# The first expert index from the two maxima, two ring buffers opened by the first output half, and the late half of an output projection ahead of a head's query and scores

## The chip, the cores and the metric

The kernel runs as one program on one core of a Trainium2 chip. Its engines are TensorE (PE, matrix products into the accumulation memory PSUM), VectorE (DVE), ScalarE (ACT), GpSimd (POOL) and SyncE (SP), each with its own queue of instructions that it works through strictly in order; they wait for one another on semaphores. Sixteen DMA engines carry the transfers. The metric is the device time of one execution in microseconds, the median of several runs.

## The reference

Two transformer blocks over 256 tokens of 1024 numbers, in float32. The end of the second one is what the change touches: a cross attention over a memory, its output projection, and a product-key expert layer.

```python
x = x + memory_cross_attention(h, m, ...)       # ends in  o @ w_o   (the stage "xo")
h = rmsnorm(x, norm_ffn_g)
def token_chunk(xc):                            # 128 tokens at a time
    q = (xc @ w_q).reshape(128, 8, 2, 128)      # 8 heads, two half queries
    s = einsum("thpd,hpnd->thpn", q, subkeys)   # 128 scores for each half
    s1, i1 = top_k(s[:, :, 0], 16)
    s2, i2 = top_k(s[:, :, 1], 16)
    cand_s = s1[..., :, None] + s2[..., None, :]        # 256 sums
    cand_i = i1[..., :, None] * 128 + i2[..., None, :]
    top_s, top_pos = top_k(cand_s, 16)
    e = take_along_axis(cand_i, top_pos)        # 16 experts of 16384
    g = softmax(top_s)
    a = gelu(einsum("td,thkd->thk", xc, w_down[e]))
    return einsum("thk,thkd->td", g * a, w_up[e])
```

The largest of the 256 sums is always the sum of the two largest scores, so its index is the pair of their indices.

## The kernel before

All products of the dense stages are made from split operands (a high and a low part, three products for one). The 256 tokens are two halves of 128, m = 0 and m = 1. The expert layer is 16 steps `it`, eight heads of the first half and then eight of the second; each step has 16 picks. A pick is a number n = 16 it + k, 256 in all. For each pick GpSimd issues one gather (`indirect_dma_start`, line 2711): 128 tokens fetch one row of 2048 numbers each (the expert's down and up vectors), 1.05 MB, into one of a ring of buffers R. Three things are then done with a gathered buffer, two buffers (one group g) at a time:

- `dot_rows` on VectorE multiplies the down half with the token's row XN and sums (instruction `CUSTOM_DVE_ANT_0`, line 2497);
- ScalarE takes the GELU (`act_d`, line 1595), VectorE multiplies with the gate (`coef`, line 2506), and ScalarE makes a diagonal matrix of it (`DIAG`, line 1607);
- TensorE adds diagonal times up half to the output (`sums`, line 1167) and raises `up_done`.

`free_slot(n)` has GpSimd wait before gather n. The table `OPENED` names the picks that take a buffer for the first time, with the semaphore count that says that its old content is read; all other picks reuse the buffer of an earlier pick and wait for `up_done` of that one. Picks 0 to 7 are in `OPENED`; pick 8 reuses the buffer of pick 0 and so on, so that pick 19 waits for the sum of pick 12. Seven buffers go round until pick 21 opens another one.

The beginning of step 0 lies among the last dense work, and its order is written out by hand on each engine. The names in it: `side("xo", AXo, g, 1)` is half g of the output projection of the second token half (line 1019, 12 matrix products), it needs the low part AXo_lo of the attention result (VectorE, line 2291, after AXo_hi by ScalarE); `query(j, 0, ...)` is the query of head j (line 641, eight products for each part named) and `head_scores(j, 0)` on TensorE its scores (line 656, label SK,QP), which first wait until ScalarE has copied the query out (`queries(j, 0)`, QP, line 1615); `head_scores` on ScalarE copies the scores into SC (line 1582; line 1619 for head 0). On VectorE `first_eight` and `second_eight` pick the experts of step 0 and write their indices IDX (line 2411), `top_a` to `top_h` do that for the later steps, and `residual_side`, `gain_side` and `mean_side` are the norm of the second token half. On ScalarE `square_side`, `gate_exp`, `gelu`, `diagonals` and `activate` (the last two together) belong to the same.

Of the kernel before, what the change touches and what calls it, by code (L numbers as in the profile page):

```python
# [17 lines left out]
T = 256  # L18
# [152 lines left out]
def build(nc, weights, vecs, consts, xT, x, mem, rows, gws, gbs, subkeys, experts, out):  # L171
    ctx = ExitStack()
    with ctx:
# [115 lines left out]
        for n, u in enumerate((1, 2, 5, 6, 12)):  # L289
            OPENED[3 + n] = (u, XO_END)  # L290
# [284 lines left out]
        def _(pe):  # L575
# [575 lines left out]
            query(1, 0, (1,))  # L1151
            head_scores(1, 0)
            has_lo(pe, *values_parts(1))
            side("xo", AXo, 0, 1)
            side("xo", AXo, 1, 1)
            query(2, 0)
# [56 lines left out]
        def _(act):  # L1213
# [400 lines left out]
            def queries(j, m):  # L1614
# [4 lines left out]
            drain_aux(act.activation(SC[:, 0, 0:2, :], v3(batch(act, *scores_of(0, 0))[:, 0:T], 2), ACT.Copy),  # L1619
                      *scores_of(0, 0))  # L1620
# [5 lines left out]
            queries(1, 0)  # L1626
            head_scores(1, 0)
            gate_exp(0)
            warm(ACT.Gelu_apprx_tanh)
            gelu(0, 0)  # L1630
            queries(2, 0)
            diagonals(0, 0)
            head_scores(2, 0)
            square_side("xo", 3, 1, 0)
# [60 lines left out]
        def _(dve):  # L1695
# [723 lines left out]
            def decode_eight(ks, side):  # L2419
# [19 lines left out]
                index(0, ks)  # L2439
# [10 lines left out]
            def first_eight():  # L2450

                wait_aux(dve, *scores_of(0, 0))
                for vals, idx, src, work in firsts(0):
                    st.do(dve.max(vals[:, 0:8], src))
                st.sync()
                for vals, idx, src, work in firsts(0):
                    st.do(dve.max_index(idx[:, 0:8], vals[:, 0:8], src))
                st.then(sums_of(c8[:, 0, :].rearrange("p (a b) -> p a b", b=8), low8, low8))
                st.do(dve.tensor_copy(tif[:, :, 0:8], ti[:, :, 0:8]))
                st.then(dve.max(cv[:, 0:8], c8[:, 0, :]))  # L2460
                st.then(dve.max_index(cp[:, 0, 0:8], cv[:, 0:8], c8[:, 0, :]))
                decode_eight(low8, 8)

            def second_eight():

                st.do(dve.match_replace(c8[:, 1, :], cv[:, 0:8], c8[:, 0, :], LOWEST))
                for vals, idx, src, work in firsts(0):
                    st.do(dve.match_replace(work, vals[:, 0:8], src, LOWEST))
                st.sync()
# [45 lines left out]
            top_a(1)  # L2515
            top_b(1)
# [5 lines left out]
            coefs(0, 1)  # L2522
            gain_side(1, 1, 0)
# [164 lines left out]
        def _(pool):  # L2688
# [14 lines left out]
            for it in range(16):  # L2703
                pool.wait_ge(idx_ready, it + 2 if it else 1)
                for k in range(TOPK):
                    if it == 0 and k == 8:
                        pool.wait_ge(idx_ready, 2)
# [93 lines left out]
```

## Time and profile before

| | |
|---|---|
| median of the runs (lowest, highest) | 1336.57 us (1336.38, 1337.8) |
| profiled execution, first to last instruction | 1332.9 us |
| TensorE busy | 1212.4 us (91%) |
| VectorE busy | 935.0 us (70%) |
| ScalarE busy | 544.3 us (41%) |
| GpSimd busy | 292.8 us (22%) |
| DMA | 396.71 MB, mean 298 GB/s |
| chain that ended last | PE 56%, DMA 32%, DVE 6%, ACT 3% |
| mean granted TensorE clock | 0.986 of full speed |

No time of its own is given for the profiled execution but its span of 1332.9 us; the median lies 3.67 us above that span. Busy shares are means over a program with very different stages; the stages are told apart by the slices of the page's second part and by windows. The chain is followed back from the last instruction, at each step to what released it.

### The profile page before, as it was taken

How to read it: one execution, taken by the hardware profiler on the slowest of the kernel's cores; microseconds unless marked ns; L12 is line 12 of the kernel's file. 1: busy time of each engine (PE TensorE's matmuls, PEld its weight loads, DVE VectorE, ACT ScalarE, POOL GpSimd, SP SyncE). 2: the span in 40 equal slices, each digit the busy share in tenths (PEclk: the TensorE clock that was granted, in tenths of full speed). 3: DMA queues.
4: the chain of work that ended last, by engine and by line, in shares of the span. 5: the costliest groups of instructions: out<-in, count | busy, mean ns of one | idle time of the engine just before them, and what ended most of it. 6: DMA issues, size and time to landing. Idle time of an engine off the chain costs nothing.

```text
span 1332.9 us, 17294 instructions
## 1 busy us (share of the span) xinstructions
PE 1212.4 (91%) x6222; PEld 874.1 (66%) x6222; DVE 935.0 (70%) x1853; ACT 544.3 (41%) x977; POOL 292.8 (22%) x261
## 2 busy tenths in 40 slices
PE   9999999999999999999998999899877877877776
PEld 9999998988888899999774554444422323332332
DVE  6865758887764675557687787776777777777655
ACT  5843225556643446645643333233322222222312
POOL 0000000000000000000034455444544444544430
PEclk9999999999999999999999999999999999999999
DMA  7553225555565654447779999999999999999996
GB/s 281 190 184 133 95 102 211 194 172 189 190 227 199 206 177 172 143 171 288 281 278 420 420 418 420 418 420 419 420 420 419 420 421 419 420 419 421 420 420 267
DMA packets 55927, 396.71 MB, mean 298 GB/s; under 512 B 6320, under 2 KB 6320, under 8 KB 8624
## 3 DMA queue, kind: packets, MB, share of 16 engines
q0 software_dynamic: 36864, 268.45, 48.7%
q1 hardware_dynamic: 17136, 119.16, 25.0%
q10 hardware_dynamic: 1856, 8.13, 1.7%
q8 instruction: 47, 0.77, 0.2%
q14 instruction: 24, 0.20, 0.0%
HBM read 394.67 MB, written 1.05 MB: 297 GB/s over the span
## 4 chain that ended last, share of the span: by engine, by line
PE 56%; DMA 32%; DVE 6%; ACT 3%; issue 2%; POOL 2%; DVEq 0%; ACTq 0%; POOLq 0%
DMA R<-experts,IDX 32%; PE ps L591 19%; PE ps L674 10%; PE ps L1167 8%; PE ps L904 4%; PE ps L603 3%; PE ps L906 2%; PE ps L641 2%; POOL R L2711 2%; PE ps L1019 1%; DVE R L2497 1%; PE ps L799 1%; PE ps L787 1%; ACT DIAG L1607 1%; PE ps L1046 1%
## 5 line engine op out<-in xcount | busy, mean ns | idle before, releaser
L1167 PE MATMUL ps<-R,DIAG 128*128 128x512 f32 x1020 | 482.4, 620 | 105.2 <-ACT DIAG L1607 105.2
L1167 PEld LDWEIGHTS ps<-R,DIAG 128*128 128x128 f32 x1020 | 190.2, 195 | 372.9 <-issue 196.2
L2497 DVE CUSTOM_DVE_ANT_0 R<-R,XN 128x1024 f32<-128x1024 f32 x256 | 313.5, 1226 | 142.8 <-DMA R<-experts,IDX 142.2
L2711 POOL DMA_INDIRECT R<-experts,IDX x256 | 291.5, 1139 | 531.7 <-PE ps L1167 273.0
L1738 DVE TENSOR_TENSOR w_lo<-raw,w_hi 128x1024 fp32r<-128x1024 f32 x204 | 241.7, 1220 | 78.5 <-ACT w_hi L1220 74.3
L1220 ACT ACTIVATE w_hi<-raw 128x1024 fp32r<-128x1024 f32 x203 | 204.7, 1051 | 77.4 <-DMA raw<-weights 77.4
L1595 ACT ACTIVATE act_d<-dots,rst 128x2 f32<-128x2 f32 (+1 forms) x130 | 38.5, 296 | 329.9 <-DVE dots L2497 329.8
L1607 ACT ACTIVATE DIAG<-con,coef 128x128 f32<-128x128 f32 x255 | 88.6, 394 | 122.2 <-DVE coef L2506 120.9
L591 PE MATMUL ps<-opA_lo,w_hi 128*128 128x256 f32 x384 | 110.6, 288 | 0.5 <-issue 0.5
L591 PE MATMUL ps<-opA_hi,w_lo 128*128 128x256 f32 x384 | 108.5, 283 | 0.0
L591 PE MATMUL ps<-opA_hi,w_hi 128*128 128x256 f32 x384 | 108.5, 283 | 0.0
L591 PE MATMUL ps<-both_C,w_hi 128*128 128x256 f32 x576 | 105.4, 284 | 1.3 <-DVE MB L1958 1.0
L2691 POOL TENSOR_SCALAR_AFFINE_SELECT WS<-WS 128x1024 f32<-128x1024 f32 x1 | 1.1, 1085 | 466.7 <-DMA BS<-gbs 466.7
L591 PEld LDWEIGHTS ps<-both_C,w_hi 128*128 128x128 f32 x576 | 90.3, 192 | 3.2 <-DVE MB L1958 1.8
L904 PE MATMUL ps<-both_C,w_hi 128*128 128x512 f32 x256 | 89.0, 392 | 0.9 <-DVE both_C L1708 0.9
L591 PE MATMUL ps<-both_C,w_lo 128*128 128x256 f32 x288 | 81.5, 283 | 0.0
L591 PEld LDWEIGHTS ps<-opA_lo,w_hi 128*128 128x128 f32 x384 | 73.5, 191 | 1.7 <-issue 0.8
L591 PEld LDWEIGHTS ps<-opA_hi,w_lo 128*128 128x128 f32 x384 | 73.6, 192 | 0.0
L591 PEld LDWEIGHTS ps<-opA_hi,w_hi 128*128 128x128 f32 x384 | 73.5, 191 | 0.0
L906 PE MATMUL ps<-both_C,w_lo 128*128 128x256 f32 x256 | 71.7, 280 | 0.0
L904 PEld LDWEIGHTS ps<-both_C,w_hi 128*128 128x128 f32 x256 | 47.9, 187 | 11.6 <-issue 1.2
L591 PEld LDWEIGHTS ps<-both_C,w_lo 128*128 128x128 f32 x288 | 55.3, 192 | 0.0
(396 smaller groups left out, 1757.1 us busy)
## 6 DMA issues: line engine op xcount, KB each, us to landing
raw<-weights SPq DMA_DIRECT2D x103, 1024.0 KB, 4.9
PQW<-weights SPq DMA_DIRECT2D x6, 1024.0 KB, 8.5
R<-experts,IDX POOLq DMA_INDIRECT x256, 29.9
LNR<-rows ACTq DMA_DIRECT2D x3, 1024.0 KB, 4.9
raw<-weights SPq DMA_DIRECT2D x4, 512.0 KB, 8.7
XF<-xT SPq DMA_DIRECT2D x2, 512.0 KB, 5.7
MEM<-mem ACTq DMA_DIRECT2D x1, 1024.0 KB, 7.8
XR<-x ACTq DMA_DIRECT2D x1, 1024.0 KB, 5.0
```

The source lines that it names most:

```text
L591: mm = pe.matmul(dst[:, c * T:(c + 1) * T], a[:, i, c * P:(c + 1) * P], b[:, k0 + i, :], start=(first and c == 0 and i == ks[0] and n == 0 ...
L603: mm = pe.matmul(dst[:, m * 256:(m + 1) * 256], b[:, k0 + i, m * P:(m + 1) * P], a[:, i, :], start=(first and m == 0 and i == ks[0] and n ...
L674: mm = pe.matmul(psum[:, 4 + 2 * g + m, :], o[:, 4 * k + i, m * P:(m + 1) * P], a[:, 2 * i:2 * i + 2, :].rearrange("p a b -> p (a b)"), st ...
L904: pe.matmul(dst[:, c, :], w_up[:, k, c * P:(c + 1) * P], both_C[:, :, k, :], start=(k == 0), stop=False, skip_group_check=True)
L906: mm = pe.matmul(dst[:, c, 0:T], w_down[:, k, c * P:(c + 1) * P], both_C[:, 0, k, :], start=False, stop=(k == 7), skip_group_check=True)
L1167: mm = pe.matmul(psum[:, 4 + 2 * m + n, :], DIAG[:, k, :], rows_[:, D + n * 512:D + (n + 1) * 512], start=(it % 8 == 0 and k == 0), stop=True,
L1220: act.activation(w_hi[s][:, 4 * h:4 * h + 4, :], raw[s][:, 4 * h:4 * h + 4, :], ACT.Copy).then_inc(hi_ready, 1)
L1595: act.activation(act_d[:, par, k0:k1], dots[:, par, k0:k1], ACT.Gelu_apprx_tanh, scale=rst[:, it // 8:it // 8 + 1]).then_inc(gelu_done, 1)
L1607: ins = act.activation(DIAG[:, k, :], ident, ACT.Copy, scale=coef[:, par, k:k + 1])
L1738: dve.tensor_tensor(w_lo[w][:, ks, :], raw[w][:, ks, :], w_hi[w][:, ks, :], ALU.subtract).then_inc(lo_ready, 1)
L2497: dve.tensor_tensor_reduce(out=rows_[:, 0:D], in0=rows_[:, 0:D], in1=XN[:, m, :], scale=1.0, scalar=0.0, op0=ALU.mult, op1=ALU.add, accum_ ...
L2711: pool.indirect_dma_start(out=R[u][:, :], out_offset=None, in_=experts, in_offset=bass.IndirectOffsetOnAxis(ap=IDX[:, it, k:k + 1], axis=0 ...
```

## The change

Four edits, all at the start of the expert layer. (1) `first_eight` reads the scores of head 0 directly from PSUM, where before ScalarE copied them to SC; that copy is gone. It writes the index of pick 0 from the two maxima's indices at once and those of picks 1 to 7 afterwards, and takes the two `match_replace` of `second_eight` over. GpSimd waits for the one index before pick 0, for the seven before pick 1, and for the eight before pick 8. (2) `OPENED`: the buffers in units 1 and 5 open with the first half of the "xo" projection, and take picks 3 and 4; units 2, 6 and 12 still wait for both halves. (3) On TensorE both halves `side("xo", AXo, 0, 1)` and `side("xo", AXo, 1, 1)` come ahead of the second part of head 1's query and of its scores. (4) ScalarE does `gate_exp(0)`, `gelu(0, 0)` and a `square_side` before it copies head 1's query, and VectorE does `top_a(1)` and `top_b(1)` after the first two pairs of dot products, where they stood ahead of both.

```diff
-        for n, u in enumerate((1, 2, 5, 6, 12)):
-            OPENED[3 + n] = (u, XO_END)
+        FIRST_XO_END = half_end(BLOCK["xo"])
+        s0 = BLOCK["xo"] % 4
+        for n, u in enumerate((s0, 4 + s0)):
+            OPENED[3 + n] = (u, FIRST_XO_END)
+        for n, u in enumerate((s0 + 1, 5 + s0, 12)):
+            OPENED[5 + n] = (u, XO_END)
...
             query(1, 0, (0,))
             cross_values(1)
-            query(1, 0, (1,))
-            head_scores(1, 0)
             has_lo(pe, *values_parts(1))
             side("xo", AXo, 0, 1)
             side("xo", AXo, 1, 1)
+            query(1, 0, (1,))
+            head_scores(1, 0)
             query(2, 0)
             query(3, 0, (0,))
             head_scores(2, 0)
...
             queries(0, 0)
-            drain_aux(act.activation(SC[:, 0, 0:2, :], v3(batch(act, *scores_of(0, 0))[:, 0:T], 2), ACT.Copy),
-                      *scores_of(0, 0))
...
             values_hi(1)
-            queries(1, 0)
-            head_scores(1, 0)
             gate_exp(0)
             warm(ACT.Gelu_apprx_tanh)
             gelu(0, 0)
+            square_side("xo", 3, 1, 0)
+            queries(1, 0)
+            diagonals(0, 0)
+            head_scores(1, 0)
             queries(2, 0)
-            diagonals(0, 0)
             head_scores(2, 0)
-            square_side("xo", 3, 1, 0)
             activate(0, 1)
...
             def first_eight():
-                wait_aux(dve, *scores_of(0, 0))
-                for vals, idx, src, work in firsts(0):
+                pa = batch(dve, *scores_of(0, 0))
+                lists = [(vals, idx, pa[:, q * NK:(q + 1) * NK], work)
+                         for q, (vals, idx, _, work) in enumerate(firsts(0))]
+                for vals, idx, src, work in lists:
...
+                st.do(dve.tensor_copy(tif[:, :, 0:8], ti[:, :, 0:8]))
                 st.then(sums_of(c8[:, 0, :].rearrange("p (a b) -> p a b", b=8), low8, low8))
+                largest = slice(0, 1)
+                dve.scalar_tensor_tensor(out=IDX[:, 0, largest], in0=tif[:, 0, largest], scalar=float(NK),
+                                         in1=tif[:, 1, largest], op0=ALU.mult, op1=ALU.add
+                                         ).then_inc(idx_ready, 1)
...
-                decode_eight(low8, 8)
+                decode_eight(low8, 8, slice(1, 8))
+                for vals, idx, src, work in lists:
+                    st.do(dve.match_replace(work, vals[:, 0:8], src, LOWEST))
+                st.sync()
+                drain_aux(dve.engine_nop(), *scores_of(0, 0))
...
-            top_a(1)
-            top_b(1)
             dot_rows(0, 0)
             residual_side("xo", 3, 1, 0)
             coefs(0, 0)
             dot_rows(0, 1)
             residual_side("xo", 4, 1, 1)
             coefs(0, 1)
+            top_a(1)
+            top_b(1)
             gain_side(1, 1, 0)
...
-                pool.wait_ge(idx_ready, it + 2 if it else 1)
+                pool.wait_ge(idx_ready, it + 3 if it else 1)
                 for k in range(TOPK):
-                    if it == 0 and k == 8:
-                        pool.wait_ge(idx_ready, 2)
+                    if it == 0 and k in (1, 8):
+                        pool.wait_ge(idx_ready, 2 if k == 1 else 3)
```

On VectorE the order after the gates GW of step 0 was this: MAX to MAX_INDEX are `top_a(1)` and `top_b(1)`, `ISA R,dots` is a dot product with a gathered buffer.

```order
L2490 TENSOR_SCALAR GW<-gx,gs 128x16
L2359 MAX tv<-SC 128x8 x2
L2362 MATCH_REPLACE sW<-tv,SC 128x128 x2
L2368 MAX tv<-sW 128x8
...
L2372 MAX_INDEX ti<-tv,sW 128x8 x2
L2497 ISA R_150,dots<-R_150,XN 128x1024
...
L2506 TENSOR_TENSOR coef<-act_d,GW 128x2
...
L2247 TENSOR_TENSOR XN<-XR,LNR 128x512 x2
L2378 CAST tif<-ti 128x32
```

With the change the same place reads:

```order
L2500 TENSOR_SCALAR GW<-gx,gs 128x16
L2507 ISA R_150,dots<-R_150,XN 128x1024
...
L2507 ISA R_140,dots<-R_140,XN 128x1024
L2507 ISA dots 128x1
L2244 TENSOR_TENSOR XR<-XR,ps 128x512
L2516 TENSOR_TENSOR coef<-act_d,GW 128x2
L2361 MAX tv<-SC 128x8 x2
L2364 MATCH_REPLACE sW<-tv,SC 128x128 x2
...
L2249 TENSOR_TENSOR XN<-XR,LNR 128x512 x2
```

The selection work of step 1 moved behind the coefficients of the second pair (the second `coef`, the last one shown ahead of MAX). On ScalarE, from the high part of the attention result on, the order was:

```order
L1534 ACTIVATE AXo_hi<-ps 128x4x128
L1615 ACTIVATE QP<-ps 128x2x128
L1582 ACTIVATE SC<-ps,rst 128x256
L1587 ACT_TABLE_LOAD
L1587 ACTIVATE gx,gs<-cv,gs,rst 128x16
L1384 ACT_TABLE_LOAD
L1384 ACTIVATE lbd<-con 128x1
L1595 ACTIVATE act_d<-dots,rst 128x2
```

and it is now:

```order
L1538 ACTIVATE AXo_hi<-ps 128x4x128
L1591 ACT_TABLE_LOAD
L1591 ACTIVATE gx,gs<-cv,gs,rst 128x16
L1388 ACT_TABLE_LOAD
L1388 ACTIVATE lbd<-con 128x1
L1599 ACTIVATE act_d<-dots,rst 128x2
L1490 ACTIVATE XS,ssq<-XR 128x512
L1619 ACTIVATE QP<-ps 128x2x128
L1611 ACTIVATE DIAG<-con,coef 128x128 x2
L1586 ACTIVATE SC<-ps,rst 128x256
L1619 ACTIVATE QP<-ps 128x2x128
L1586 ACTIVATE SC<-ps,rst 128x256
```

The copy of head 1's query, QP, moved behind the first GELU (act_d) and a square (XS). On TensorE, after the attention values (XT,VX), only the place of head 1's second query part and scores differs; they now stand behind the last "xo" product and ahead of head 2's query (PQW_130):

```order
L1023 MATMUL ps<-w_hi_61,AXo_hi 128x512
L645 MATMUL ps<-H_129,raw_51 128x128 x8
L660 MATMUL ps<-SK,QP 128x128 x2
L645 MATMUL ps<-H_129,PQW_130 128x128 x16
L645 MATMUL ps<-H_129,PQW_131 128x128 x8
L660 MATMUL ps<-SK,QP 128x128 x2
L1171 MATMUL ps<-R_150,DIAG 128x512 x2
```

What moved there are eight products and two; the sums of pick 0 (R_150) stay behind all of them.

## Rows read from the trace of the kernel before

**Rows 1.** The page, its second part: GB/s moved in 40 equal slices.
```profile
GB/s 281 190 184 133 95 102 211 194 172 189 190 227 199 206 177 172 143 171 288 281 278 420 420 418 420 418 420 419 420 420 419 420 421 419 420 419 421 420 420 267
```

**Rows 2.** The page, DMA queues: packets, MB, share of 16 engines' span.
```profile
q0 software_dynamic: 36864, 268.45, 48.7%
```

**Rows 3.** The chain that ended last, its end: start us, us, what.
```profile
1290.64 33.21 DMA R<-experts,IDX
1323.87 1.23 DVE R L2497
```

**Rows 4.** Windows of one us: busy times of PE, PEld, DVE, ACT, POOL, clock, DMA share, GB/s.
```profile
676.00:677.00 1.00, 0.53 (x5) 0.40 (x4) 0.96 (x7) 0.38 (x1) 0.90 (x1) 1.00 0.72 131
...
685.00:686.00 1.00, 1.00 (x12) 1.00 (x11) 0.97 (x2) 0.00 (x0) 0.69 (x2) 1.00 0.64 221
```

**Rows 5.** Timeline of GpSimd: start us, us, line, what, idle before and releaser.
```profile
674.57 1.09 POOL L2711 DMA_INDIRECT R<-experts,IDX  x1 [206.22 <-DVE IDX L2411]
...
683.06 0.94 POOL L2711 DMA_INDIRECT R<-experts,IDX  x1 [4.92 <-PE ps L1019]
...
692.01 0.95 POOL L2711 DMA_INDIRECT R<-experts,IDX  x1 [1.60 <-PE ps L1167]
...
722.36 0.94 POOL L2711 DMA_INDIRECT R<-experts,IDX  x1 [2.57 <-PE ps L1167]
```

**Rows 6.** Timeline of VectorE: dot products that waited for their gather.
```profile
700.59 1.23 DVE L2497 CUSTOM_DVE_ANT_0 R<-R,XN 128x1024 f32<-128x1024 f32 x1 [0.63 <-DMA R<-experts,IDX]
...
730.52 1.23 DVE L2497 CUSTOM_DVE_ANT_0 R<-R,XN 128x1024 f32<-128x1024 f32 x1 [1.01 <-DMA R<-experts,IDX]
```

**Rows 7.** Timeline of VectorE from the first pick to the third pair.
```profile
670.35 0.49 DVE L2454 MAX8 tv<-SC 128x8 f32<-128x128 f32 x2 [1.58 <-ACT SC L1619]
...
671.22 0.28 DVE L2457 FIND_INDEX8 ti<-tv,SC 128x8 uint32<-128x128 f32 x1
...
674.12 0.17 DVE L2411 SCALAR_TENSOR_TENSOR IDX<-ef 128x8 uint32<-128x8 f32 x1
675.08 0.69 DVE L2291 TENSOR_TENSOR AXo_lo<-ps,AXo_hi 128x512 fp32r<-128x512 f32 x1 [0.80 <-ACT AXo_hi L1534]
...
682.41 0.49 DVE L2359 MAX8 tv<-SC 128x8 f32<-128x128 f32 x2 [0.20 <-DVE GW L2490]
...
685.28 1.23 DVE L2497 CUSTOM_DVE_ANT_0 R<-R,XN 128x1024 f32<-128x1024 f32 x1
...
691.38 0.16 DVE L2506 TENSOR_TENSOR coef<-act_d,GW 128x2 f32<-128x2 f32 x1
...
694.18 1.23 DVE L2497 CUSTOM_DVE_ANT_0 R<-R,XN 128x1024 f32<-128x1024 f32 x1
```

**Rows 8.** Timeline of ScalarE, from head 0's scores to head 3's.
```profile
669.94 0.39 ACT L1619 ACTIVATE SC<-ps 128x256 f32<-128x256 f32 x1 [0.80 <-PE ps L656]
...
687.76 0.30 ACT L1595 ACTIVATE act_d<-dots,rst 128x2 f32<-128x2 f32 x1 [6.11 <-DVE dots L2497]
...
689.56 0.62 ACT L1486 ACTIVATE XS<-XR 128x512 f32<-128x512 f32 x1
...
703.17 0.45 ACT L1582 ACTIVATE SC<-ps,rst 128x256 f32<-128x256 f32 x1
```

**Rows 9.** The chain that ended last, TensorE's pieces: start us, us, what.
```profile
677.32 5.49 PE ps L1019 x24
...
889.34 5.40 PE ps L1167 x8
```

**Rows 10.** Timeline of TensorE: queries (L641) and sums (L1167).
```profile
682.63 5.52 PE L641 MATMUL ps<-H,PQW 128*128 128x128 f32 x48
...
689.24 7.13 PE L1167 MATMUL ps<-R,DIAG 128*128 128x512 f32 x16 [0.15 <-ACT DIAG L1607]
...
698.15 3.70 PE L1167 MATMUL ps<-R,DIAG 128*128 128x512 f32 x8
...
709.66 3.70 PE L1167 MATMUL ps<-R,DIAG 128*128 128x512 f32 x8 [1.77 <-ACT DIAG L1607]
```

More of the change, by code:

```diff
@@ L2417, in top_g, with decode_eight @@
                 index(it, slice(0, 16))
-            def decode_eight(ks, side):
+            def decode_eight(ks, side, listed=None):
                 shape, bits = [P, 8, side], {8: 3, 16: 4}[side]
@@ L2438, in decode_eight @@
                 st.sync()
-                index(0, ks)
+                index(0, listed or ks)
             def sums_of(dst, rs, cs):
@@ L2450, in first_eight, with second_eight @@
             def first_eight():
-                wait_aux(dve, *scores_of(0, 0))
-                for vals, idx, src, work in firsts(0):
+                pa = batch(dve, *scores_of(0, 0))
+                lists = [(vals, idx, pa[:, q * NK:(q + 1) * NK], work)
+                         for q, (vals, idx, _, work) in enumerate(firsts(0))]
+                for vals, idx, src, work in lists:
                     st.do(dve.max(vals[:, 0:8], src))
                 st.sync()
-                for vals, idx, src, work in firsts(0):
+                for vals, idx, src, work in lists:
                     st.do(dve.max_index(idx[:, 0:8], vals[:, 0:8], src))
+                st.sync()
+                st.do(dve.tensor_copy(tif[:, :, 0:8], ti[:, :, 0:8]))
                 st.then(sums_of(c8[:, 0, :].rearrange("p (a b) -> p a b", b=8), low8, low8))
-                st.do(dve.tensor_copy(tif[:, :, 0:8], ti[:, :, 0:8]))
+                largest = slice(0, 1)
+                dve.scalar_tensor_tensor(out=IDX[:, 0, largest], in0=tif[:, 0, largest], scalar=float(NK),
+                                         in1=tif[:, 1, largest], op0=ALU.mult, op1=ALU.add
+                                         ).then_inc(idx_ready, 1)
                 st.then(dve.max(cv[:, 0:8], c8[:, 0, :]))
                 st.then(dve.max_index(cp[:, 0, 0:8], cv[:, 0:8], c8[:, 0, :]))
-                decode_eight(low8, 8)
-            def second_eight():
-                st.do(dve.match_replace(c8[:, 1, :], cv[:, 0:8], c8[:, 0, :], LOWEST))
-                for vals, idx, src, work in firsts(0):
+                decode_eight(low8, 8, slice(1, 8))
+                for vals, idx, src, work in lists:
                     st.do(dve.match_replace(work, vals[:, 0:8], src, LOWEST))
                 st.sync()
+                drain_aux(dve.engine_nop(), *scores_of(0, 0))
+            def second_eight():
+                st.then(dve.match_replace(c8[:, 1, :], cv[:, 0:8], c8[:, 0, :], LOWEST))
                 st.do(dve.tensor_copy(cand[:, 0:8, 0:8], c8[:, 1, :].rearrange("p (a b) -> p a b", b=8)))
```

## The prediction

> **What bounds the kernel now.** I read the slices first. From about the twenty-second on they stand at 418 to 421 GB/s [rows 1], which nothing earlier in the kernel reaches: from the expert layer's start to its end the DMA engines are full. The gathers' queue moves 268.45 MB [rows 2], 256 gathers of 1.05 MB; at 420 GB/s that is 639 us, 2.50 us for a gather. Then the end of the chain: the last gather is issued at 1290.64 and its dot product starts at 1323.87, 33.21 us of pure transfer [rows 3]. So the time is the moment when the gather stream starts, plus 639 us, plus every stretch in which the stream runs dry, plus a short tail. Ahead of the stream the chain is TensorE's, but only what moves the stream counts.
>
> The first window with gather traffic is 676 to 677, 131 GB/s [rows 4]; the first gather was issued at 674.57 [rows 5], so bytes move about 1.8 us after the issue. One gap follows, 221 GB/s in the window 685 to 686 [rows 4]: gathers 0 to 2 were out, and pick 3 was issued only at 683.06, after the "xo" projection [rows 5]. After that the stream lives off its ring. GpSimd waits for TensorE's sums before nearly every gather [rows 5], and how much reserve it has shows where a dot product waits for data: gather 19, issued at 722.36 [rows 5], landed just before 730.52 [rows 6], 8.16 us later. Gather 7 landed just before 700.59 [rows 6], so twelve gathers took 29.93 us, 2.494 each: no hole. What would the 8.16 us be at least, in an empty queue? For gather 0 they are 1.8 us to the first byte, and 1.05 MB have moved only after some 3.2 us more (131 GB/s in its first window), 5.0 us as the lower bound. From above: the dots of the second pair ran at 688.4 to 690.7 without a wait for data, which holds gather 3, issued at 683.06, under 6.5 us. I take 5.8, nearer the upper end, since the last of sixteen engines decides. The reserve at pick 19 is then 2.3 us (1.7 to 3.1). By the same reading picks 8 to 14 have more, and picks 15 and 17 about 0.3 us more.
>
> **The change at the front: 2.7 us earlier.** Without the copy of 0.39 us at 669.94 [rows 8] the maxima, which waited for it [rows 7], start at 669.96. The finds end 1.15 us after the maxima's start (671.22 + 0.28 against 670.35) [rows 7]; a cast, the sums and the one index instruction of 0.17 us follow, some 0.3 us ahead of it: the index at 671.4 instead of 674.12, gather 0 at 671.9 instead of 674.57 [rows 5]. The other seven indices come at about 673.9, gather 1 at 674.3, in time for the end of gather 0's bytes. Reading PSUM instead of SBUF I cost at nothing. The Trainium skill, "Perfetto Trace Analysis", Optimizing Scalar/DVE Operations, gives VectorE about 60 ns of overhead on SBUF and 125 ns on PSUM; by it the front would be some 0.3 us later, an estimate from that page, and the forecast the same.
>
> **The two buffers and the projection: one gap less.** AXo_lo is done at 675.77 (675.08 + 0.69) [rows 7], bound by ScalarE as before. TensorE starts "xo" at about 675.95, 1.4 us earlier than 677.32, and needs the same 5.49 us [rows 9]: first half done at 678.7, second at 681.4. Picks 3 and 4 go at 679 and 680.2, picks 5 to 7 from 681.7, with gathers 0 to 2 still moving. The gap at 685 goes, 0.2 to 0.7 us. If nothing else happened, the stream would be about 2.7 us ahead, a little more with the gap.
>
> **What pays for it: the sums of the first step come later.** I follow the three engines by their order.
> - VectorE: `second_eight` lost two match_replace, 0.5 us, and `top_a(1)`, `top_b(1)` (682.41 to 685.28, 2.87 us) stand no more ahead of the dots [rows 7]. The first dot starts at 681.9 instead of 685.28, the GELU at 687.76 - 3.4 = 684.4 [rows 8].
> - ScalarE: now the GELU, and then the square stand ahead of head 1's query copy. The square waits for the residual after the second dot, 684.2 + 0.7 = 684.9, and takes 0.7 us with its read-out (0.62 the instruction) [rows 8]. QP starts at 685.6, before at 676.2.
> - TensorE: "xo" ends at 681.4, the query part at 683.2, and then it stands until QP is done: head 1's scores at 686.05. Behind them are three query parts, 5.52 us [rows 10] less their overlap, so 5.4, and head 2's scores, 0.45 us each: 686.05 + 0.45 + 5.4 + 0.45 = 692.35 for the first sum, against 689.24 [rows 10]. **3.1 us later.**
> - The second pair: ScalarE's GELU of it stands behind its copy of head 2's scores, 691.9 + 0.8 + 0.4 = 693.1, and the coefficient comes at 693.4, not 691.38 [rows 7]. Behind that coefficient VectorE had 2.8 us of work until the third pair's dot at 694.18 [rows 7]; now it also has the 2.87 us. The third pair's dots start at 693.4 + 2.8 + 2.87 = 699.05, **4.9 us later**.
> - From dot to sum took 694.18 to 698.15 [rows 7, 10], of it 0.3 us waiting for data that now lie there: sums at 702.8, 4.65 later. The fourth pair waited 0.63 us for gather 7 [rows 6], which falls away: 4.0 later. ScalarE's copy of head 3's scores at 703.17 [rows 8] moves to 707.1, and from it a fixed series of table loads, root, exponential and GELU led to TensorE's sums at 709.66 [rows 8, 10], 6.49 us: now 713.6, **3.9 us later**.
> - From there to pick 12's sum TensorE is full (sums, query, sums, query), so pick 19 is issued at 722.36 + 3.9 = 726.3.
>
> **The sum.** Pick 19 lands at 726.3 + 5.8 = 732.1 instead of 730.5: 3.9 later less 2.3 reserve, **1.6 us later**, and the stream is dense behind it, since pick 21 opens another buffer and the reserve grows. The 2.7 us of the front are used up before: gather 8 waits for the first sum, 692.01 + 3.1 = 695.1 [rows 5], while gathers 0 to 7 are over by about 697 minus the engines' spread, so some engines stand empty. The same sum by the bounds of the floor is 3.9 - 3.1 = 0.8 and 3.9 - 1.7 = 2.2. An error of half a us in the 3.9 widens this to 0.3 to 2.7. Span: 1332.9 + 1.6 = 1334.5. The median lies 3.67 us above the span shown, so 1336.57 + 1.6 = 1338.2. What a measurement of this kernel can tell from no change is about 0.2%, 2.7 us; 1.6 us is within it.
>
> **Rivals.**
> - The head start arrives whole, -2.7 to -3.4 us, 1333.5. That needs picks 15 to 19 no later than now by 0.4 us, so an error of 4.3 us in the chain above. For it speaks that the first dots really come 3.4 us earlier. Against it, TensorE's wait for QP follows from the written order and leaves nothing to chance. The Trainium skill, "Perfetto Trace Analysis", Optimization Strategy, says to find the gaps of the saturated resource and to make what they depend on start sooner. Taken alone that is this case, and by it the time is 1333.5. Chance 0.12.
> - The sums come later, but by no more than 1.9 to 2.7 us at pick 19 (TensorE or ScalarE catch up, or the floor of a gather is nearer 5.0 us): the end moves by -0.4 to +0.3, 1336.5. Chance 0.2.
> - Slower beyond the bound: the shift at pick 19 passes 5.0 us, the point from which 5.0 - 2.3 = 2.7 is lost. One mechanism would do it. TensorE now stands idle twice in 12 us, 1.6 us before "xo" and 2.9 us before head 1's scores, and the clock row shows what a drop costs: at 889.34 eight sum products took 5.40 us [rows 9], where they take 3.70 [rows 10]. One such stretch in the dense part before pick 12 adds 1.7 us, 3.3 in all, 1339.9. The Trainium skill, "TensorE: Matmul & The Clock Gate", The HAM clock gate, says that activity releases the throttle and idleness brings it back; against it, no row before 840 us shows less than full clock, though TensorE waits there too (1.77 us at 709.66) [rows 10]. Without the clock, a restart of all sixteen engines at each hole (the ramp of rows 4) adds up to 0.5 us a hole. Chance together 0.23.
> - The forecast, +0.3 to +2.7 us: chance 0.45.
>
> **How the numbers follow.** Faster by over 0.2% is the first rival alone, 0.12. Slower by over 0.2% is the third with the upper rim of the forecast, 0.25. The rest, 0.63, is within 0.2%. The range must leave out no more than 2 in 10: from 1335.2, which cuts the first rival, to 1340.2, which holds the clock's case and cuts what is beyond.
>
> **What the next profile would show.** Right: the first gather issued at about 671.9, picks 3 and 4 near 679 and 680; TensorE's L660 for head 1 near 686.0 behind a wait of some 2.9 us for QP; the first sum near 692.3; the third pair's dots near 699; windows between 694 and 707 with less than 420 GB/s; pick 19 near 726.3. Wrong: if the first sum stands before 690, the order costs less than I say; if the windows after 677 are all full, the head start arrives; if the clock is under 1.00 before 730, the third rival holds; if gathers in an empty queue land in under 5 us, the reserve was larger.

## The result, and the profile after

The changed kernel took 1342.85 us in the median (1342.58 to 1343.23, 4 runs), the kernel before on the same chip 1336.53: a ratio of 1.0043 with an interval of 1.0031 to 1.0055, so 4.1 to 7.4 us slower. Forecast were 1338.2 us and a range up to 1340.2. The profiled execution spans 1341.5 us. All medians and ratios here are of fast runs; one execution of front_open, below, took 2680.8 us, twice the time, and is left out.

One thing has to be set right before the two traces are laid side by side. In the profile after, head 0's scores start at 670.87 us, in that of before they started at 669.19, though nothing ahead of them was changed. A second profile of the kernel before has them at 669.09, and over all 18 profiles of this study they start either at 668.8 to 669.4 (ten) or at 670.6 to 671.0 (eight), kernels before and after in both groups. So 1.68 us of the 8.6 us between the two spans are chance. It also explains about half of the 3.67 us by which the median of the kernel before stood above the span shown: the second profile, with the same span of 1332.9 us, took 1334.63 us itself, so both executions profiled were of the faster kind. From here on, times are compared **from the start of head 0's scores on TensorE** ("from the scores").

TensorE in the changed kernel, from its timeline (start us, us, line, what, count, idle time before and its releaser; L660 are a head's scores, L1023 "xo", L645 queries, L1171 sums; in the kernel before these were L656, L1019, L641 and L1167):

```profile
670.87 0.71 PE L660 MATMUL ps<-SK,QP 128*128 128x128 f32 x4 [0.47 <-ACT QP L1619]
...
677.57 0.50 PE L1023 MATMUL ps<-w_hi,AXo_lo 128*128 128x512 f32 x1 [1.54 <-DVEq L1718]
...
687.48 0.91 PE L660 MATMUL ps<-SK,QP 128*128 128x128 f32 x4 [2.39 <-ACT QP L1619]
688.18 7.00 PE L645 MATMUL ps<-H,PQW 128*128 128x128 f32 x48
...
695.47 7.03 PE L1171 MATMUL ps<-R,DIAG 128*128 128x512 f32 x16
...
716.65 3.70 PE L1171 MATMUL ps<-R,DIAG 128*128 128x512 f32 x8 [1.78 <-ACT DIAG L1611]
```

The two stands are there, 1.54 and 2.39 us. The 48 query products behind the second take 7.00 us; the same 48 took 5.52 before [rows 10]. The windows say why (us; busy of PE, PEld, DVE, ACT, POOL; granted clock, DMA share, GB/s):

```profile
687.00:688.00 1.00, 0.52 (x4) 0.52 (x5) 0.74 (x2) 1.00 (x5) 0.99 (x1) 0.93 1.00 418
688.00:689.00 1.00, 1.00 (x6) 1.00 (x6) 0.00 (x0) 0.49 (x2) 0.54 (x1) 0.50 0.99 418
...
690.00:691.00 1.00, 1.00 (x7) 1.00 (x7) 1.00 (x3) 0.00 (x0) 0.00 (x0) 0.50 0.97 410
```

The granted clock fell to 0.50, the lower of its two levels (1.2 GHz), right behind the stand. Scores to first sum: 24.60 us, before 20.05 (689.24 - 669.19) [rows 10].

GpSimd (gathers 0, 3, 8, 11 and 19) and VectorE (the first maxima, the first dot product, the first of the third pair, and that of pick 19):

```profile
673.60 1.09 POOL L2721 DMA_INDIRECT R<-experts,IDX  x1 [203.21 <-DVE IDX L2466]
...
680.86 0.94 POOL L2721 DMA_INDIRECT R<-experts,IDX  x1 [2.62 <-PE ps L1023]
...
698.13 0.94 POOL L2721 DMA_INDIRECT R<-experts,IDX  x1 [9.59 <-PE ps L1171]
...
708.11 1.50 POOL L2721 DMA_INDIRECT R<-experts,IDX  x1 [3.90 <-PE ps L1171]
...
729.35 0.94 POOL L2721 DMA_INDIRECT R<-experts,IDX  x1 [1.96 <-PE ps L1171]
```

```profile
671.62 0.50 DVE L2458 MAX8 tv<-ps 128x8 f32<-128x128 f32 x2 [1.16 <-PE ps L660]
...
683.42 1.22 DVE L2507 CUSTOM_DVE_ANT_0 R<-R,XN 128x1024 f32<-128x1024 f32 x1
...
702.17 1.22 DVE L2507 CUSTOM_DVE_ANT_0 R<-R,XN 128x1024 f32<-128x1024 f32 x1
...
737.49 1.23 DVE L2507 CUSTOM_DVE_ANT_0 R<-R,XN 128x1024 f32<-128x1024 f32 x1 [1.07 <-DMA R<-experts,IDX]
```

The first gather goes out 2.73 us after the scores, before 5.38 (674.57 - 669.19) [rows 5]: the head start is there, 2.65 us. Pick 19 goes out 58.48 us after them, before 53.17: 5.3 us later. The stream in windows of 4 us, first of the changed kernel, then of the kernel before:

```profile
692.00:696.00 4.00, 4.00 (x35) 3.76 (x34) 0.00 (x0) 0.66 (x2) 0.00 (x0) 1.00 1.01 426
696.00:700.00 4.00, 4.00 (x11) 1.80 (x10) 3.37 (x18) 1.69 (x6) 0.94 (x1) 1.00 0.37 102
700.00:704.00 4.00, 4.00 (x21) 2.61 (x20) 3.90 (x10) 0.00 (x0) 2.17 (x2) 1.00 0.86 303
...
708.00:712.00 4.00, 3.70 (x12) 1.85 (x11) 3.79 (x11) 2.72 (x6) 2.52 (x2) 1.00 0.56 178
...
724.00:728.00 4.00, 4.00 (x22) 2.74 (x21) 3.07 (x11) 0.85 (x3) 2.48 (x2) 1.00 0.99 358
728.00:732.00 4.00, 4.00 (x14) 2.03 (x13) 2.06 (x5) 0.99 (x3) 1.88 (x2) 1.00 0.94 358
```

```profile
696.00:700.00 4.00, 4.00 (x22) 2.65 (x21) 3.66 (x12) 1.37 (x4) 1.21 (x2) 1.00 1.01 426
700.00:704.00 4.00, 2.98 (x11) 1.59 (x10) 3.24 (x9) 1.71 (x5) 1.87 (x2) 1.00 1.00 416
...
708.00:712.00 4.00, 2.34 (x6) 1.14 (x7) 3.21 (x7) 1.85 (x5) 0.30 (x2) 1.00 1.02 424
```

The stream runs dry twice, behind gather 7 (pick 8 comes at 698.13) and behind gather 10 (pick 11 comes at 708.11), and is thin up to 736. From 676 to 744 the 17 windows of before sum to 6930 GB/s, those of after to 6081: 849 x 4 / 420 = 8.1 us of full stream less. By place: 1.0 us gained up to 696, then 4.2 lost by 704, 0.3 by 708, 2.3 by 712, 2.3 by 736. Less the 1.68 us of chance, and less the 0.35 us of bytes that the changed kernel moved ahead of 676 (147 GB/s from 675 to 676), it is 6.1, the size of the result. From 744 on both run at full rate until the last ten us.

### The profile page after: what moved, and what is told of

Its sections match the earlier page's. It is cut to its first block, busy times and chain, and to the rows that moved or that the text cites. A ratio compares the mean times of both kernels' runs of the same rounds, so it can differ in the third digit from the quotient of the medians.

```text
span 1341.5 us, 17294 instructions
## 1 busy us (share of the span) xinstructions
PE 1211.9 (90%) x6222; PEld 873.8 (65%) x6222; DVE 936.0 (70%) x1854; ACT 543.7 (41%) x976; POOL 290.2 (22%) x261
## 3 DMA queue, kind: packets, MB, share of 16 engines
HBM read 394.67 MB, written 1.05 MB: 295 GB/s over the span
## 4 chain that ended last, share of the span: by engine, by line
PE 57%; DMA 30%; DVE 7%; ACT 3%; issue 2%; POOL 0%; DVEq 0%; ACTq 0%; POOLq 0%
DMA R<-experts,IDX 30%; PE ps L595 19%; PE ps L678 10%; PE ps L1171 9%; PE ps L908 4%; PE ps L607 3%; PE ps L645 3%; PE ps L910 2%; DVE R L2507 1%; PE ps L803 1%; PE ps L1023 1%; PE ps L791 1%; ACT DIAG L1611 1%; PE ps L1050 1%; PE ps L1077 1%
## 5 line engine op out<-in xcount | busy, mean ns | idle before, releaser
L1171 PE MATMUL ps<-R,DIAG 128*128 128x512 f32 x1020 | 478.6, 615 | 110.7 <-ACT DIAG L1611 107.7
L1171 PEld LDWEIGHTS ps<-R,DIAG 128*128 128x128 f32 x1020 | 188.1, 194 | 376.8 <-issue 197.5
```

What stands on the lines that cost most here:

```text
L1171: mm = pe.matmul(psum[:, 4 + 2 * m + n, :], DIAG[:, k, :], rows_[:, D + n * 512:D + (n + 1) * 512], start=(it % 8 == 0 and k == 0), stop=True,
```

## The experiments

For every run two times are given, both from the scores: when pick 19 is issued, and when the last gather has landed (the last DMA row of the chain, its start plus its length). For the kernel before, profiled again (TensorE, GpSimd, and the chain's last piece of DMA), and for the changed kernel's chain:

```profile
669.09 0.71 PE L656 MATMUL ps<-SK,QP 128*128 128x128 f32 x4 [0.47 <-ACT QP L1615]
...
722.34 0.94 POOL L2711 DMA_INDIRECT R<-experts,IDX  x1 [2.57 <-PE ps L1167]
...
1290.42 33.35 DMA R<-experts,IDX
```

```profile
1299.03 33.36 DMA R<-experts,IDX
```

So 53.25 and 1323.77 - 669.09 = 654.68 for before; 58.48 and 1332.39 - 670.87 = 661.52 for the changed kernel. The others, in the order of pick 19 (shift against this second profile of before, us; ratio of times to before with its interval where timed in rounds):

| kernel | first sum | pick 19 | end | ratio |
|---|---|---|---|---|
| query_later | -0.6 | -3.0 | -2.3 | 0.9987 (0.9978, 0.9996) |
| front_open | -0.6 | -1.6 | -1.6 | 0.9987 (0.9978, 0.9996) |
| before_late | +1.7 | +0.5 | +0.3 | 1.0009 (1.0000, 1.0018) |
| old_pe_act | -0.8 | +0.8 | +1.3 | 1.0015 (1.0006, 1.0024) |
| mid_2us | 0.0 | +1.5 | +2.5 | 1.0016 (1.0006, 1.0025) |
| qp_first | +1.1 | +1.7 | +2.2 | 1.0012 (1.0003, 1.0021) |
| filled_short | +2.9 | +3.6 | +3.8 | 1.0030 (1.0020, 1.0039) |
| after_again | +2.9 | +3.6 | +4.7 | 1.0034 (1.0021, 1.0048) |
| mid_4us | 0.0 | +3.6 | +3.7 | 1.0030 (1.0019, 1.0041) |
| changed kernel | +4.6 | +5.2 | +6.8 | 1.0043 (1.0031, 1.0055) |
| filled | +4.7 | +5.4 | +5.9 | 1.0044 (1.0031, 1.0058) |
| orders_only | +5.4 | +6.0 | +6.4 | 1.0045 (1.0031, 1.0059) |

**before_again**: the kernel before, unchanged.

> The kernel before, unchanged, for a second profile. The profile shown of before had head 0's scores (TensorE, L656) at 669.19, that of the changed kernel at 670.87, although nothing ahead of them was changed. Theory A: that is a difference between executions; this profile has the scores anywhere from 669 to 671, a span near 1334.8, and a time near 1336.5. Theory B: the changed program itself is slower up to there; then the scores stand at 669.2 again. From the scores to the first sum 20.05 us by both.

Measured: one run of 1334.63 us, scores at 669.09, first sum 20.05 us after them. By itself it did not settle whether the 1.68 us were chance; it fell on the same side as the first profile. The later ones settled it: before_late and mid_4us, which are the kernel before up to that point, have 670.97 and 670.83, and the changed kernel's third and fourth profile 669.28 and 669.39. Theory A.

**front_open**: edits 1 and 2 without the orders. On TensorE, ScalarE and VectorE the changed kernel's new orders are put back, for example

```diff
             cross_values(1)
+            query(1, 0, (1,))
+            head_scores(1, 0)
             has_lo(pe, *values_parts(1))
             side("xo", AXo, 0, 1)
             side("xo", AXo, 1, 1)
-            query(1, 0, (1,))
-            head_scores(1, 0)
```

> Edits 1 and 2 alone: the early first index and the two buffers opened by the first half of xo; all three engines' orders as before. Theory A (the orders alone cost the time, the head start is worth what the reserve of picks 15 to 19 allows): first gather 2.7 us earlier in relation to head 0's scores, first sum 0.5 us earlier, time 1336.5 - 1.9 = 1334.6. Theory B (the head start is lost in any case, since the later picks are issued no earlier): 1336.5 less 0.5, 1336.0. Theory C (part of the loss of the changed kernel comes from these edits): above 1337.5.

Measured: 0.9987, some 1.7 us faster (0.5 to 2.9). Its gathers 0 and 19, with the scores at 669.28:

```profile
672.01 1.09 POOL L2721 DMA_INDIRECT R<-experts,IDX  x1 [203.44 <-DVE IDX L2466]
...
720.89 0.94 POOL L2721 DMA_INDIRECT R<-experts,IDX  x1 [1.87 <-PE ps L1171]
```

The first gather is 2.65 us earlier, pick 19 1.64, and the end 1.6: the end moved as pick 19 did. Theory A; these two edits cost nothing and bring part of their head start.

**orders_only**: edits 3 and 4 on the kernel before, the first index and the buffers as they were.

> Edits 3 and 4 alone, the orders of TensorE, ScalarE and VectorE; the first index and the buffers as before. First sum some 25.1 us after head 0's scores (20.05 before) if the clock falls, 23.6 if not. Theory A (the end follows pick 19's issue one for one whatever the stream did ahead of it): the end 5 to 6 us later, ratio 1.004. Theory B (the head start of edits 1 and 2 emptied the queue that would have covered the late sums; without it a reserve of 2.3 us holds): 3 us later, ratio 1.0025.

Measured: 1.0045. Its two rows on TensorE, head 1's scores and the queries behind them:

```profile
688.46 0.71 PE L656 MATMUL ps<-SK,QP 128*128 128x128 f32 x4 [3.20 <-ACT QP L1615]
689.01 7.15 PE L641 MATMUL ps<-H,PQW 128*128 128x128 f32 x48
```

The orders alone cost as much as the whole change; in this profile the clock fell here too (7.15 us for the 48 products). Theory B, in which the reserve would have covered 2.3 us of it, falls.

**qp_first**: ScalarE copies head 1's query ahead of the first GELU.

```diff
             gate_exp(0)
             warm(ACT.Gelu_apprx_tanh)
+            queries(1, 0)
             gelu(0, 0)
             square_side("xo", 3, 1, 0)
-            queries(1, 0)
```

> The changed kernel, with head 1's query copy on ScalarE moved ahead of the first GELU; the order of TensorE and VectorE stays. The query is ready at about 685.1, the GELU waits until 685.9 anyway. Theory A (the sums are late by ScalarE's order, and the stand of 2.39 us drops the clock): head 1's scores 1.8 us earlier, the stand 0.6 us, the clock stays full, first sum 21.4 us after head 0's scores instead of 24.6, time 1339.6. If the stand of 1.54 us ahead of xo is enough for the clock: 22.8 us, 1341.1. Theory B (late sums are absorbed by the stream's reserve): no change from 1342.9.

```profile
685.49 0.71 PE L660 MATMUL ps<-SK,QP 128*128 128x128 f32 x4 [0.53 <-ACT QP L1619]
686.03 5.52 PE L645 MATMUL ps<-H,PQW 128*128 128x128 f32 x48
```

The stand is 0.53 us, the queries take 5.52 us at full clock, the first sum comes 21.1 us after the scores (21.4 expected). The time, 1.0012, is better than expected (1339.6 would be 1.0023 against 1336.5). The stand of 1.5 us ahead of "xo" is still there and dropped no clock. What remains slower, 2.2 us at the end, goes with a pick 19 that is 1.7 later.

**filled and filled_short**: products of no use in TensorE's wait for QP, twenty and nine.

```diff
             query(1, 0, (1,))
+            for n in range(9):
+                pe.matmul(psum[:, 4, 0:P], H4[:, n % 8, 0:P], H4[:, n % 8, 0:P], start=True, stop=True,
+                          skip_group_check=True)
             head_scores(1, 0)
```

> The changed kernel, with 20 extra products of 128 columns into an accumulator that the first sum overwrites, between head 1's second query part and its scores, so that TensorE works through most of its 2.39 us wait for QP. Nothing else moves. Theory A (the stand lets the clock fall, and the half clock from 687.8 to 691.2 costs 1.45 us): granted clock 1.00 in that stretch, head 0's scores to the first sum 23.15 us instead of 24.60, time 1341.4. Theory B (the clock falls whatever TensorE does there): 24.6 us again, 1342.9. Theory C (the end is set elsewhere): 23.15 us, but 1342.9.

> The changed kernel with nine extra products instead of twenty in TensorE's wait for QP (twenty took 4.63 us and overshot the wait of 2.39 us by 1.9, with the clock at 1.00). Now 2.06 us of work in a wait of 2.39 us. Theory A (the stand lets the clock fall and that costs 1.45 us): clock 1.00, head 1's scores 16.6 us after head 0's as in the changed kernel, first sum at 23.15 instead of 24.60, pick 19 and the end 1.45 us earlier, ratio to before 1.0033. Theory B (the clock costs nothing at the end): ratio 1.0043 as for the changed kernel.

Twenty were mis-sized: they took 4.63 us and moved head 1's scores from 16.61 to 18.53 us after those of head 0, which gave back what the clock had saved; that run told nothing on the time. Nine fit (L1160 here is the helper through which the extra products are recorded):

```profile
684.67 2.17 PE L1160 MATMUL ps<-H 128*128 128x128 f32 x18
687.22 0.71 PE L660 MATMUL ps<-SK,QP 128*128 128x128 f32 x4 [0.37 <-issue]
687.76 5.52 PE L645 MATMUL ps<-H,PQW 128*128 128x128 f32 x48
```

First sum at 22.95, ratio 1.0030, both near what theory A has (23.15 and 1.0033). But the next run took the force out of it.

**after_again**, and four more profiles of single executions: is the fall of the clock the change's?

> The changed kernel unchanged, for its ratio on this chip and a second profile. Head 0's scores to the first sum 24.6 us again with the half clock for some 3.4 us of them, if the fall of the clock comes from TensorE's stand and not from chance; ratio 1.004 to 1.005.

```profile
687.49 0.71 PE L660 MATMUL ps<-SK,QP 128*128 128x128 f32 x4 [2.39 <-ACT QP L1619]
688.03 5.52 PE L645 MATMUL ps<-H,PQW 128*128 128x128 f32 x48
...
693.84 7.03 PE L1171 MATMUL ps<-R,DIAG 128*128 128x512 f32 x16
```

The same kernel, the same stand of 2.39 us, and no fall: first sum at 22.96, ratio 1.0034. What was expected here, 24.6 again, did not come.

> The changed kernel, a third profile, for the clock alone. Where it falls behind the stand ahead of head 1's scores, the first sum is 24.6 us after head 0's scores, else 22.96. If the stand causes it, it falls in some executions of this kernel and in none with the stand filled.

> The changed kernel, a fourth profile: 24.6 or 22.96 us, as for the third.

> Edits 3 and 4 alone, a second profile. The stand is longer here (head 1's scores at 17.42 us behind head 0's, 16.61 in the changed kernel). First sum at 25.4 with the fall, 23.8 without. If a longer stand makes the fall surer, 25.4.

> The changed kernel with the wait for QP filled by nine products, a second profile. If the stand causes the fall of the clock, 22.95 us again from head 0's scores to the first sum and a clock of 1.00; one fall here would say that it has another cause.

First sums 24.61, 22.97, 25.30 and 22.99 us after the scores. With the stand kept (2.39 or 3.2 us) the clock fell in four profiles of six, both times in the kernel with the longer stand; with it filled or shortened in none of four. That fits a stand that makes the fall possible and not sure; with so few profiles it is not proven. Other stands bear it out: in old_pe_act TensorE stood 2.47 us (ahead of 699.37) and in before_late 2.31 (ahead of 712.00) with the clock at 1.00. And in filled_short, whose wait for QP is filled, the clock fell further on, behind a stand of 1.91 us, so that eight sum products took 5.40 us instead of 3.70 (granted clock 0.50 from 737 to 739):

```profile
734.66 5.40 PE L1174 MATMUL ps<-R,DIAG 128*128 128x512 f32 x8 [1.91 <-ACT DIAG L1614]
```

So the change's stand is not the only one that the clock can fall behind. The stream was dense by then, and this later fall cost nothing that the end shows.

**old_pe_act**: VectorE's part of edit 4 alone, with edits 1 and 2 (TensorE and ScalarE as before).

> The changed kernel with the old orders of TensorE and ScalarE: edits 1 and 2, and VectorE's selection work of step 1 behind the first two pairs of dot products. It takes VectorE's part of edit 4 by itself. Theory A: the third pair's dot products come some 2 us later than in front_open since the selection work now stands right ahead of them, pick 19's issue 2 us later, and the end with it: 1.8 us above front_open, ratio 1.0000. Theory B (TensorE's and ScalarE's orders alone do the harm): 0.9987 as front_open.

The first dot product of its third pair, and pick 19, with the scores at 668.84:

```profile
695.69 1.22 DVE L2507 CUSTOM_DVE_ANT_0 R<-R,XN 128x1024 f32<-128x1024 f32 x1
```

```profile
722.87 0.94 POOL L2721 DMA_INDIRECT R<-experts,IDX  x1 [1.97 <-PE ps L1171]
```

26.85 us after the scores, in front_open it was 24.43: the selection work put behind the first two pairs lands ahead of the third. Pick 19 is 2.4 later than in front_open, the time 1.0015 against 0.9987. Theory A, somewhat above its size. VectorE's part by itself turns the gain into a loss. TensorE's and ScalarE's orders were not run without VectorE's.

**before_late**: nine extra products ahead of the first sum of the kernel before.

```diff
             head_scores(2, 0)
+            for n in range(9):
+                pe.matmul(psum[:, 4, 0:P], H4[:, n % 8, 0:P], H4[:, n % 8, 0:P], start=True, stop=True,
+                          skip_group_check=True)
```

> The kernel before, with nine extra products (2.06 us of TensorE) ahead of the first sum, and nothing else. It measures the step that the prediction took for sure: how much later may the issues of picks 8 to 19 come until the end moves. First sum, and pick 19's issue, about 2.0 us later in relation to head 0's scores. Theory A (the recorded step, a reserve of 2.3 us at pick 19): the end moves by 0 to 0.3 us, ratio 1.0000 to 1.0002. Theory B (no reserve: the end follows pick 19's issue one for one, as in the runs so far): 2.0 us later, ratio 1.0015. Theory C (the reserve is what pick 19's first packet waits more than in an empty queue, 3.49 - 1.78 = 1.7 us): 0.3 us later.

The first sum was 1.7 later, but pick 19 only 0.5: the waits of 1.02 us ahead of sums (0,3) and around them took up the rest. Picks 8 to 12 did come 1.2 to 1.6 us later, and the end 0.3: those have a reserve of about that much. On pick 19 it says nothing, and the interval (1.0000 to 1.0018) tells none of the theories from another.

**mid_2us and mid_4us**: the same behind sums (0,4), nine and eighteen, into an idle accumulator.

```diff
             sums(0, 4)
+            for n in range(9):
+                pe.matmul(psum[:, 6, 0:P], H4[:, n % 8, 0:P], H4[:, n % 8, 0:P], start=True, stop=True,
+                          skip_group_check=True)
             query(0, 1, (0,))
```

> The kernel before with nine extra products (2.06 us, into an idle accumulator) on TensorE behind sums (0,4), where it is full up to pick 19, and nothing else; the late first sum of the run before_late was made up by TensorE's waits before it reached pick 19 (0.5 us later). Here picks 17 to 19 are issued 2.06 us later, picks 0 to 16 as before. Theory A (recorded: reserve 2.3 us at pick 19): end 0 later. Theory B (end follows pick 19 one for one): 2.06 later, ratio 1.0015. Theory C (reserve 1.7 us, the excess of the first packet's wait over an empty queue): 0.4 later, ratio 1.0003.

> The same with eighteen products, 4.12 us. Recorded reserve: 1.8 us later, ratio 1.0014. One for one: 4.1, ratio 1.0031. Reserve of 1.7 us: 2.4, ratio 1.0018. If a stream with a short queue also moves less (358 to 395 GB/s in the changed kernel's windows from 712 to 736, where its queue was never empty), some 1 us more than 2.4.

Picks 17 and 19 were 1.5 and 3.6 us later, not 2.06 and 4.12, since TensorE made up half a us; the ratios 1.0016 and 1.0030 are 2.1 and 4.0 us. Mid_4us leaves picks 0 to 16 where they were, to 0.4 us, with no clock and no order changed, and costs what the changed kernel's second profile costs. Its windows, then four windows of one us at the place where the rate drops, and picks 17 and 19 on GpSimd and VectorE:

```profile
716.00:720.00 4.00, 4.00 (x39) 4.00 (x37) 3.12 (x15) 0.99 (x3) 1.21 (x1) 1.00 1.02 422
720.00:724.00 4.00, 4.00 (x16) 2.09 (x15) 2.69 (x5) 0.00 (x0) 1.42 (x1) 1.00 0.64 264
724.00:728.00 4.00, 4.00 (x22) 2.70 (x21) 1.30 (x3) 1.26 (x4) 1.23 (x2) 1.00 0.84 281
728.00:732.00 4.00, 4.00 (x13) 1.97 (x12) 2.83 (x9) 0.73 (x3) 2.90 (x3) 1.00 1.00 406
732.00:736.00 4.00, 4.00 (x11) 1.84 (x10) 2.20 (x3) 0.62 (x2) 3.11 (x3) 1.00 0.95 334
```

```profile
722.00:723.00 1.00, 1.00 (x4) 0.47 (x3) 1.00 (x1) 0.00 (x0) 0.51 (x1) 1.00 0.52 205
723.00:724.00 1.00, 1.00 (x6) 0.52 (x5) 0.10 (x2) 0.00 (x0) 0.90 (x1) 1.00 0.04 16
724.00:725.00 1.00, 1.00 (x12) 1.00 (x11) 0.00 (x0) 0.00 (x0) 0.79 (x1) 1.00 0.76 106
725.00:726.00 1.00, 1.00 (x9) 0.76 (x8) 0.00 (x0) 0.25 (x1) 0.15 (x1) 1.00 0.62 180
```

```profile
722.49 1.42 POOL L2714 DMA_INDIRECT R<-experts,IDX  x1 [5.28 <-PE ps L1167]
...
727.71 0.94 POOL L2714 DMA_INDIRECT R<-experts,IDX  x1 [2.56 <-PE ps L1167]
```

```profile
728.70 1.23 DVE L2500 CUSTOM_DVE_ANT_0 R<-R,XN 128x1024 f32<-128x1024 f32 x1 [1.04 <-DMA R<-experts,IDX]
...
734.94 1.23 DVE L2500 CUSTOM_DVE_ANT_0 R<-R,XN 128x1024 f32<-128x1024 f32 x1 [1.80 <-DMA R<-experts,IDX]
```

Against 420 GB/s the four windows from 720 on lack 1.5, 1.3, 0.1 and 0.8 us, 3.7 in all: the end's shift. Most of it is lost ahead of pick 17 and not at pick 19: the stream runs dry between 722 and 724, just as pick 17 goes out (722.49), and is at full rate again at 726, 3.5 us after that issue (the window from 726 to 727 has 418 GB/s). Pick 17, sent into the dry queue, lands in at most 6.2 us (728.70 - 722.49). Pick 19 takes 7.23 us (734.94 - 727.71), but the queue is not empty then: picks 17 and 18 are still moving at 418 GB/s.

**query_later**: front_open, and two query parts behind the sums that pick 19 needs.

```diff
             sums(0, 4)
-            query(0, 1, (0,))
             sums(0, 5)
-            query(0, 1, (1,))
+            query(0, 1, (0,))
             sums(0, 6)
-            head_scores(0, 1)
+            query(0, 1, (1,))
             sums(0, 7)
+            head_scores(0, 1)
```

On ScalarE `activate(0, 7)` goes ahead of `queries(0, 1)` to match.

> Edits 1 and 2 alone as in the faster run front_open (ratio 0.9987), and after it the two query parts that stand ahead of sums (0,5) and (0,6) on TensorE each one place later, with head 8's scores and its query copy behind the last sums of step 0. TensorE is full from sums (0,4) on, so pick 19's issue comes about 1.5 us earlier than in front_open. Theory A (the end follows pick 19's issue until the stream is dense): 1.0 to 1.5 us less than front_open, ratio 0.9977. Theory B (the stream is bounded elsewhere, by its start): 0.9987 again.

Pick 19 came 1.4 us earlier than in front_open, the end by the trace 0.7, and the ratio is the same, 0.9987. So beyond some 1.6 us earlier the end does not follow pick 19 one for one. The windows say what bounds it then: front_open still has a dip, 342 GB/s from 724 to 728, where query_later has 393 or more in every window of 4 us from 692 to 740. With no hole left the end goes by the stream's start, as theory B has it. Both versions beat the kernel before and the changed one; front_open is the simpler.

## Why the prediction was wrong

Its direction held, and so did the chain of engines that makes the sums late; its size did not, 1.6 us forecast and 6.3 measured, because the last step from pick 19 to the end was wrong. Step by step, the forecast against the changed kernel, less the 1.68 us:

- **The front.** Gather 0 forecast at 671.9, measured 673.60 - 1.68 = 671.92. The maxima take 0.50 us from PSUM and took 0.49 from SBUF [rows 7], so costing the PSUM reads at nothing was right; the 0.3 us that the Trainium skill's figures ("Perfetto Trace Analysis", Optimizing Scalar/DVE Operations) would have added are not in this trace.
- **The two buffers.** Picks 3 and 4 forecast at 679 and 680.2; pick 3 came at 679.18.
- **The wait for QP.** Forecast at 2.9 us with head 1's scores at 686.05; measured 2.39 and 685.80. qp_first shows that ScalarE's order causes it.
- **First sum, third pair, pick 19, without the fall of the clock** (after_again, whose scores stand at 670.88, less 1.69): first sum forecast at 692.35, measured 692.15; the third pair's first dot product forecast at 699.05, measured 700.54 - 1.69 = 698.85; pick 19 forecast at 726.3, measured 727.72 - 1.69 = 726.03. The chain of three engines through 50 us was right to 0.3 us.
- **The step that failed** is "3.9 later less 2.3 reserve, 1.6 us later". The 3.9 was near (3.6 without the fall of the clock), the reserve of 2.3 us was not there. In mid_4us, where picks 17 to 19 go out 3.6 us later and nothing else is changed, the end is 3.7 later; in after_again 3.6 and 4.7, in filled_short 3.6 and 3.8. The floor of 5.8 us was not the error: a gather sent into the dry queue landed in at most 6.2 (mid_4us), and that bound still leaves about 2 of the 2.3. Pick 19 alone was never delayed.
- **Why the reserve was not there.** What was wrong is what the floor was used for. A reserve until the landing of pick 19 says nothing of the stream ahead of it, and the stream loses from the moment when bytes stop, not from the moment when a gather is late. By mid_4us, the work up to pick 16 keeps the stream full until about 722.5, 51.7 us from the scores. The kernel before issues pick 17 at 48.03 (717.12 - 669.09 in before_again), and 3.5 us pass until the full rate: an estimate of 0.1 us of reserve at pick 17, where the prediction's reading gave 0.3 us more than at pick 19. The landing of pick 19 also hides a part: it came only 2.8 us later (734.94 - 670.83 against 730.52 - 669.19 [rows 6]) while the windows lost 3.7 us of stream.
- **Holes that were not asked after.** The forecast gave sums (0,2) 4.65 us of delay and used them only on the way to pick 19. They release pick 11, which came 6.0 us later from the scores and left the second hole at 708 to 712. And each hole costs a restart: the prediction had up to 0.5 us for it, among its rivals, where the windows from 724 to 726 in mid_4us (106 and 180 GB/s) lack 1.3.
- **The clock.** It stood among the rivals ("one such stretch adds 1.7 us"), and the first profile has it, right behind the stand ahead of head 1's scores. It made the first sum 1.64 us later (24.60 against 22.96), and pick 19 by the same. The Trainium skill ("TensorE: Matmul & The Clock Gate", The HAM clock gate) says that idleness brings the throttle back; the traces agree in four profiles of six with the stand, and in none of four without, and stands of 2.47 and 2.31 us elsewhere, with no fall behind them, show that idleness of that length does not always do it. The argument against it, that TensorE waits elsewhere at full clock, was true (1.54 us here, 1.78 at 716.65) and did not exclude it.

Together, for the changed kernel as profiled: pick 19 is 5.2 us late, 3.6 from the orders and 1.6 from the clock, and the end 6.8. The windows tell where the other 1.6 us are. Summed in windows of one us from each kernel's own scores up to 80 us behind them, the stream moved less than in before_again (in us of full stream) by 5.5 in the changed kernel, 5.4 in after_look1, 3.6 in after_again, 3.8 in filled_short and 3.5 in mid_4us; their ends are later by 6.8, 5.3, 4.7, 3.8 and 3.7. Between there and the last 20 us the stream is full in all of them. So 1.3 us of the first profile, and 1.1 of after_again, arise at the very end, while the rate dies away: from the window in which it falls below 400 GB/s for good to the last landing it takes 8.5 us in the changed kernel (from 653 us after the scores), and 7.7 in before_again (from 647). Why that tail differs between executions stays open. The head start bought little: orders_only, without it, is no slower beyond the measurement (1.0045 against 1.0043), though its pick 19 is 0.8 us later.

## What to carry to other kernels

A queue that is full at the end of a stage is no proof of reserve: ask of every issue on the way, not only of the last, how late it may come, count the time from an issue to the full rate, and read the reserve where the resource's own windows of GB/s drop, not where a consumer waits for a landing. To measure it, put idle work of a known length ahead of the issue in the kernel before; that costs one run and needs no theory. And when a reordering brings a saturated stream forward, what counts is the latest issue that still depends on the old chain: here VectorE's reordering alone moved pick 19 by 2.4 us, more than the 1.6 that the front had won, all three together by 6.0, and only the kernels that dropped the orders and kept the front were faster.

## What the runs showed of the hardware

- The same 48 products took 5.52 us or 7.00 to 7.15, by whether the granted clock fell to 0.50 behind a stand of 2.4 or 3.2 us; in the same kernel it fell in some executions and not in others. It fell once behind 1.91 us (filled_short), and not behind 2.47 (old_pe_act).
- Work ahead of the change, the same in all kernels, ended at one of two times 1.7 us apart, by execution.
- A gather of 1.05 MB, issued as the queue ran dry, landed in at most 6.2 us, and the stream was back at its full rate 3.5 us after the issue (mid_4us, pick 17); at 420 GB/s the same bytes take 2.5.
